# Stick-breaking attention with long and short query tiles paired in cycles, on one Trainium2 core

## The reference, cut to what matters

```python
u = rmsnorm(h, attn_norm_g)
q, k, v = split(u @ w_in)                      # 8 heads x 64
for each block of 128 queries (t0, t1 = t0 + 128):
    z = q[t0:t1] @ k[:t1].T * 64 ** -0.5
    strict = key index < query index
    sp = where(strict, softplus(z), 0)
    excl = reversed_cumsum(sp) - sp
    a = where(strict, exp(log_sigmoid(z) - excl), 0)
    out[t0:t1] = a @ v[:t1]
```

## Time and profile before

| what | us |
|---|---|
| median of three runs (4183.0 to 4185.79) | 4183.62 |
| the profiled execution, its own time | 4179.88 |
| its span, first to last instruction | 4178.1 |
| PE busy over the span | 3749.1 (90%) |
| ACT busy | 1303.3 (31%) |
| DVE busy | 1785.5 (43%) |
| POOL busy | 1304.8 (31%) |
| mean granted TensorE clock | 0.934 |

### The profile page before, as it was taken

How to read it: one execution, slowest core, us unless ns; L and a number is a source line. 1 busy time by engine, 2 the same in 40 slices (tenths; PEclk the granted TensorE clock), 3 DMA queues, 4 the chain that set the end, 5 groups by cost and what they waited for, 6 DMA issues and landing times. The chain is left out here.

```text
span 4178.1 us, 49886 instructions
## 1 busy us (share of the span) xinstructions
PE 3749.1 (90%) x17244; PEld 2990.7 (72%) x17244; DVE 1785.5 (43%) x3304; ACT 1303.3 (31%) x2355; POOL 1304.8 (31%) x777
## 2 busy tenths in 40 slices
PE   6877579688999999499999999998798999999897
PEld 4666556377888887378888888887686777768576
DVE  4555543424333323445555656565404233232332
ACT  3555423201011101245555555555301202020210
POOL 2110020013333332156555565655332221213031
PEclk8888589898999999699999999999898999999998
DMA  3111100122111110332443222520412111102051
GB/s 111 41 25 25 32 24 11 66 85 62 45 50 45 50 50 13 93 42 50 46 53 51 39 38 38 38 35 16 145 62 101 36 55 30 60 25 70 27 175 65
DMA packets 218590, 221.97 MB, mean 53 GB/s; under 512 B 12912, under 2 KB 174960, under 8 KB 218496
## 3 DMA queue, kind: packets, MB, share of 16 engines
q1 hardware_dynamic: 194160, 153.11, 16.9%
q10 hardware_dynamic: 24336, 67.64, 4.8%
HBM read 178.72 MB, written 33.62 MB: 51 GB/s over the span
## 5 line engine op out<-in xcount | busy, mean ns | idle before, releaser
L1191 POOL TENSOR_SCALAR even_probs<-even_probs,even_stat 128x128 f32<-128x128 f32 (+7 forms) x256 | 442.1, 1734 | 330.8 <-DVE even_stat L1568 330.8
L502 PE MATMUL ps<-all_u_hi,even_w_hi 128*128 128x512 f32 x1024 | 426.3, 416 | 24.7 <-POOL even_w_lo L1183 24.7
L506 PE MATMUL ps<-all_u_hi,even_w_lo 128*128 128x512 f32 x1024 | 403.2, 394 | 0.0
L505 PE MATMUL ps<-all_u_lo,even_w_hi 128*128 128x512 f32 x1024 | 400.9, 392 | 0.0
L455 POOL CAST odd_w_hi<-odd_w_raw 128x1024 fp32r<-128x1024 f32 x80 | 89.4, 1117 | 895.1 <-PE ps L502 686.7
L1573 DVE TENSOR_TENSOR even_probsT_lo<-ps,even_probsT_hi 128x512 fp32r<-128x512 f32 (+3 forms) x384 | 213.3, 556 | 280.2 <-ACT even_probsT_hi L1422 278.4
L502 PE MATMUL ps<-all_u_hi,odd_w_hi 128*128 128x512 f32 x768 | 305.5, 398 | 5.6 <-DVE ret_yT L2577 3.7
L505 PE MATMUL ps<-all_u_lo,odd_w_hi 128*128 128x512 f32 x768 | 303.2, 395 | 0.0
L506 PE MATMUL ps<-all_u_hi,odd_w_lo 128*128 128x512 f32 x768 | 303.1, 395 | 0.0
L1413 ACT ACTIVATE even_probs<-even_probs,even_stat 128x128 f32<-128x128 f32 (+7 forms) x256 | 199.1, 778 | 315.1 <-DVE even_stat L1562 315.1
L502 PEld LDWEIGHTS ps<-all_u_hi,even_w_hi 128*128 128x128 f32 x1024 | 194.5, 190 | 59.3 <-POOL even_w_lo L1183 25.1
(11 more groups left out here) (395 smaller groups left out, 8571.3 us busy)
## 6 DMA issues: line engine op xcount, KB each, us to landing
even_w_raw<-in_even_w_in_dram SPq DMA_DIRECT2D x64, 512.0 KB, 8.5
odd_w_raw<-in_odd_w_in_dram SPq DMA_DIRECT2D x48, 512.0 KB, 3.8
mlp_w_raw<-in_w_up_dram SPq DMA_DIRECT2D x32, 512.0 KB, 4.0
mlp_w_raw<-in_w_down_dram SPq DMA_DIRECT2D x32, 512.0 KB, 3.7
scratch_h<-residual SPq DMA_DIRECT2D x2, 4096.0 KB, 17.3
even_bias<-scratch_negc ACTq DMA_DIRECT2D x16, 512.0 KB, 6.7
scratch_yt<-even_yT ACTq DMA_DIRECT2D x32, 256.0 KB, 2.0
we_y_raw<-scratch_yt ACTq DMA_DIRECT2D x16, 512.0 KB, 4.3
```

The source lines that it names most:

```text
L502: ins = nc.tensor.matmul(dst, lh, rh, start=first, stop=False)
L505: nc.tensor.matmul(dst, lh, rl, start=False, stop=False)
L506: return nc.tensor.matmul(dst, ll, rh, start=False, stop=last)
L1191: nc.gpsimd.tensor_scalar(PB[g % 2][:, at], PB[g % 2][:, at], inv[:, s:s + 1], None, ALU.mult)\
```

## The change

`pair_stage` goes and `stick_stage` takes its place; the order of the units becomes k, q, v. No stage behind it is edited.

- **Cycles.** The two kinds of query tile of a head are paired: long rows 4, 5, 6, 7 (5 to 8 key tiles) with short rows 3, 2, 1, 0 (4 to 1 key tiles). A cycle is one long and one short row, 9 key tiles in all; a pair of heads has 8 cycles, the stage 32. The cycles run on over the borders of heads and pairs, and all is written out, without a hardware loop.
- **Three half-turns.** A cycle has three turns h: the long row's tiles 1 to 4, its tiles 5 to 8, and the short row. All go through one PSUM bank (`T`), and ACT alone copies them out, into a ring of three buffers.
- **Asked ahead.** Scores and `soft` of the long row stand two cycles ahead, of the short row one cycle; `probs` of the long row one cycle ahead. Long rows have two PSUM areas of two banks, the short row one bank.
- **Dense eighths.** Dense work for the next pair is cut into 24 eighths of 6 matmuls, one for each turn of the 24 in a pair (two at turns 2 and 5, none at 22 and 23).
- **High and low parts.** The eight DMAs go. ACT writes the high part of k to the other half of the partitions and the high part of q to the same half, DVE writes q's low part, POOL writes k's high part and its low part; the low part of k is zero on the other half.
- **Rows and v.** The short and long rows gather in one bank and ACT takes them out every second cycle (four copies a pair; before, 16 on DVE). v has two buffers and is turned through the dense bank, at the last two turns of the pair before. The rows go out by two DMAs for a pair.

```diff
-    def pair_stage(stage, kinds, rounds, weight, units, bases, w=None):
+    def stick_stage(stage, rounds, weight, bases, w):
...
+        SL = [ps[:, 0:2, :].rearrange("p b c -> p (b c)"), ps[:, 2:4, :].rearrange("p b c -> p (b c)")]
+        SS = ps[:, 4, :]
+        T = ps[:, 5, :]
+        O = ps[:, 6, :]
         DENSE = ps[:, 7, :]
...
+        def rows_of(long, c):
+            return 4 + c % 4 if long else 3 - c % 4
...
+        PIECES = [1] * STEPS
+        PIECES[2] = PIECES[5] = 2
+        PIECES[22] = PIECES[23] = 0
...
             @block.gpsimd
             def _(pool):
...
+                    nc.gpsimd.tensor_copy(KHH[m, hh, :], KN[m, :]).then_inc(doubled.sem, 1)
+                    pool.wait_ge(doubled.sem, doubled.at(n + 1))
+                    nc.gpsimd.tensor_tensor(KLO[m, hh, :], KN[m, :], KHH[m, hh, :].bitcast(F32), ALU.subtract)\
+                        .then_inc(doubled.sem, 1)
...
             @block.tensor
             def _(pe):
...
+                def turn(h):
+                    long, c, js = blocks_of(h)
+                    if js[0] == 0:
+                        pe.wait_ge(probs_ready.sem, probs_ready.at(index(long, c) + 1))
+                    if h:
+                        pe.wait_ge(probs_out_act.sem, probs_out_act.at(h))
+                    for i, j in enumerate(js):
+                        last = nc.tensor.transpose(T[:, i * P:i * P + P], probs_of(long, c)[:, j * P:j * P + P], ident[:])
+                    last.then_inc(probs_turned.sem, 1)
...
+                for e in range(4 * ND):
+                    eighth(0, e, ps[:, e // 4, :])
+                pe.wait_ge(dense_out.sem, dense_out.at(ND))
+                pe.wait_ge(step_pool.sem, step_pool.at(2))
+                scores(LONG, 0)
+                scores(LONG, 1)
+                scores(SHORT, 0)
+                turn_v(0, 0)
+                turn_v(0, 1)
+                for h in range(3 * NCY):
+                    c, k = divmod(h, 3)
+                    nxt = following(h)
+                    turn(h)
+                    if k == 0 and exists(c + 2):
+                        scores(LONG, c + 2)
+                    if k == 2 and exists(c + 1):
+                        scores(SHORT, c + 1)
+                    if h and k != 1:
+                        weigh(h - 1)
+                    for e in eighths_at(h) if nxt else ():
+                        if e % 4 == 0:
+                            pe.wait_ge(dense_out.sem, dense_out.at(ND * nxt + e // 4))
...
+                        eighth(nxt, e, DENSE)
+                    if k == 1:
+                        weigh(h - 1)
+                    if nxt and h % STEPS >= STEPS - 2:
+                        turn_v(nxt, h % STEPS - (STEPS - 2))
+                weigh(3 * NCY - 1)
...
             @block.scalar
             def _(act):
...
-                def duplicate(pair):
-
-                    act.wait_ge(dense_out.sem, dense_out.at(nd * pair + 4))
-                    for src, dst in ((QN, Q2), (KN, K2)):
-                        for hh in range(2):
-                            for part in range(2):
-                                act.dma_start(dst[part * SB_DIM:(part + 1) * SB_DIM, hh, :],
-                                              src[hh * SB_DIM:(hh + 1) * SB_DIM, :]).then_inc(doubled.sem, 16)
...
+                for n in range(ND):
+                    take_half(0, n, ps[:, n, :])
+                    if n == 1:
+                        split_of(0, 0, 0)
+                    elif n == 3:
+                        split_of(0, 0, 1)
+                soft(LONG, 0)
+                soft(LONG, 1)
+                soft(SHORT, 0)
+                split_of(0, 1, 0)
+                split_of(0, 1, 1)
+                probs(LONG, 0)
+                for h in range(3 * NCY):
+                    c, k = divmod(h, 3)
+                    nxt = following(h)
+                    s = h % STEPS
+                    if nxt and s:
+                        for e in eighths_at(h - 1):
+                            if e % 4 == 3:
+                                take_half(nxt, e // 4, DENSE)
+                    probs_out(h)
+                    if k == 0:
+                        if exists(c + 2):
+                            soft(LONG, c + 2)
+                        if exists(c + 1):
+                            probs(LONG, c + 1)
+                    elif k == 1:
+                        if c % 2 == 0 and c:
+                            rows_out(c - 1)
+                        probs(SHORT, c)
+                    elif exists(c + 1):
+                        soft(SHORT, c + 1)
+                    if nxt and s in (9, 14, 21, 22):
+                        split_of(nxt, s // 21, (9, 14, 21, 22).index(s) % 2)
+                    if s == 3 and h >= STEPS:
+                        store(h // STEPS - 1)
+                rows_out(NCY - 1)
+                store(rounds - 1)
...
             @block.vector
             def _(dve):
...
+                for h in range(3 * NCY):
+                    c, k = divmod(h, 3)
...
+                    if k == 0:
+                        later(SHORT, c)
+                    elif k == 1:
+                        if exists(c + 2):
+                            later(LONG, c + 2)
+                    if nxt and s == 15:
+                        split_lo_of(nxt, 0)
+                    if nxt and s >= STEPS - 2:
+                        v_rows(nxt, s - (STEPS - 2))
+                    if nxt and s == STEPS - 1:
+                        split_lo_of(nxt, 1)
...
-    bases = [0, SB_WIDTH, 2 * SB_WIDTH]
+    bases = [SB_WIDTH, 0, 2 * SB_WIDTH]
...
-    pair_stage("sb", ["sb"], SB_HEADS // 2, one(w_in), "qkv", [bases], w=w)
+    stick_stage("sb", SB_HEADS // 2, one(w_in), bases, w)
```

More of the change, by code:

```diff
@@ L638, in _ @@
+                split_keys(0, 0)
+                split(1, 0)
+                split_keys(0, 1)
+                split(1, 1)
+                split(1, 2)
+                for p in range(1, rounds):
+                    split(p + 1, 0)
+                    split_keys(p, 0)
+                    split(p + 1, 1)
+                    split_keys(p, 1)
+                    split(p + 1, 2)
             @block.tensor
             def _(pe):
-                if not ahead:
-                    w_open_pe(pe, w, opening=False)
@@ L643, in quarter, with eighth @@
-                def quarter(pair, i, dst):
-                    n, part = i // 2, i % 2
-                    u, half = halves[n]
-                    if half == 0 and part == 0:
-                        w_arrived(pe, w, pair, per, u)
+                def eighth(p, e, dst):
+                    n, piece = e // 4, e % 4
+                    u, half = n // 2, n % 2
+                    if half == 0 and piece == 0:
+                        w_arrived(pe, w, p, per, u)
                     tiles = w_tiles(w, u)
@@ new lines, in scores @@
+                def scores(long, c):
+                    hh = head_of(c)
+                    if long and c % 4 == 0:
+                        g = c // 4
+                        pe.wait_ge(split_hi.sem, split_hi.at(2 * g + 2))
+                        pe.wait_ge(split_lo.sem, split_lo.at(g + 1))
+                        pe.wait_ge(doubled.sem, doubled.at(2 * g + 2))
+                    before = c - 2 if long else c - 1
+                    if before >= 0:
+                        pe.wait_ge(scores_taken.sem, scores_taken.at(index(long, before) + 1))
+                    qt = rows_of(long, c)
+                    S, at, n = scores_of(long, c), slice(qt * P, qt * P + P), width(long, c)
+                    for c0 in range(0, n, HALF):
+                        c1 = max(min(c0 + HALF, n), c0 + 2 * P)
+                        nc.tensor.matmul(S[:, c0:c1], QHL[:, hh, at], KHH[:, hh, c0:c1], start=True, stop=False)
+                        nc.tensor.matmul(S[:, c0:c1], QHL[:, hh, at], KLO[:, hh, c0:c1], start=False, stop=True)
+                    nc.tensor.matmul(S[:, n - P:n], ident16[:], mask_strict[:], start=False, stop=True,
+                                     skip_group_check=True).then_inc(scores_ready.sem, 1)
```

585 lines of the change are left out of this document (210 added, 375 removed).

## The result

The changed kernel takes **4084.95 us** (median of four runs, 4084.06 to 4086.41) against 4183.31 us (4179.57 to 4185.79, four runs) for the kernel before on the same chip. The ratio is 0.9765, with a 95% interval of 0.975 to 0.9781: 98 us less, where 91 were forecast. The profiled execution has a time of its own of 4084.06 and a span of 4082.3, which is 95.8 us less than the span before.

The account below looks back on a forecast made before the run. A ring of hand-overs, with no engine full, was taken as the bound. Start 95, 24 dense cycles 242, last pair 77 and 1 for the end give 415 us: saving 91, time 4092, range 4052 to 4132.

Parts of the forecast that it names:

- The dense cycle: One of 24 cycles with dense work: 10.1 us, bounded by PE's floor of 8.6 and by 12.1.
- the ring: PE from short turn to long scores, 3.8 us, then ACT to `probs` short, 4.6; with hand-overs and short turn 8.85.
- high parts: In dense cycles, three of four high parts fall behind a long `soft` on ACT: 0.4 us a cycle.
- turn 10's wait: The next eighth waits for a dense half's take behind `probs` long, delaying the short turn: 0.25 us a cycle.
- doubled eighths: The doubled eighths at turns 2 and 5 lie in the serial part: 0.35 us a cycle.
- The last pair: Eight cycles without dense work: 7.5 us each at full clock, 10.1 at half; 9.6 taken, 77 us in all.
- What was costed at nothing: Single turn bank, POOL's splits of k, two row DMAs, and `later` with 3.9 us of slack a cycle: no cost.
- POOL: Some 2 us lost per POOL operation beside a DVE scan, five a pair: at most 1.3 us a cycle, within slack.
- A: Hand-overs vanish, PE at full clock bounds: dense cycle 8.7 us, saving 141, time 4043; chance 0.13 with what lies towards it.
- B: Asking ahead gains little and the clock dips as now: dense cycle 12.1 us, saving 32, time 4152; chance 0.22.
- C: Clock falls to half in dense cycles and stays: 17 us a cycle, slower by 75, time 4259; chance 0.035.
- D: The new order has no effect, 107 us a pair stays: only 4183 would come out; chance 0.015.

Follow-up runs that it names:

- e2: Changed kernel with six more dense eighths a pair moved from behind the long row's second half to the short turns: 4116.42 us.
- e12: e9 without its 96 unread matmuls in the last pair, everything else alike: 4045.89 us, ratio 0.967 to the kernel before.
- e7: Kernel before, with the eight DMAs of each pair issued from SP's queue instead of ACT's: 4163.42 us.
- e9: Changed kernel with rows copied before `probs` long, halves taken early, `probs` short first, high parts moved, no eighths at short turns, 96 unread matmuls: 4041.68 us.
- e10: Changed kernel with three of a pair's four high parts on ACT moved to turns without a long `soft` before them: 4074.89 us.
- e4: Changed kernel with a dense half that ends in a cycle's first turn copied out in that turn, before `probs` long: 4080.20 us.
- e5: Changed kernel with `probs` of the short row made before `probs` of the next long row: 4066.67 us.
- e6: Changed kernel with 96 matmuls that nobody reads added on PE in the last pair: 4076.21 us.
- e8: Changed kernel with DVE running each long row's scan twice: 4100.05 us.

## Why the prediction was right, step by step

- **What bounds the kernel.** That the order of the hand-overs between PE and ACT sets the time, and not the amount of work: e2 shows it for the changed kernel (+31.5 us from order alone), and e12 from the other side, 39 us quicker with the same work. For the kernel before it is read from the waits, and e7 tests one piece of it.
- **The dense cycle**, forecast 10.1 (bounds 8.6 to 12.1), measured 10.14: 243.4 us for 24 in place of 242. The hit is partly luck, since the cycle is not made up as drawn. The prediction closes the ring where PE waits for `probs` short, and in the dense cycles that wait is 0.5 us in all. PE stops elsewhere, for the take of a dense half (8.0), for the bank of the rows (6.4) and for the turned v (5.3): 20.6 us, 0.86 a cycle. The waits for the rows' bank and for v have no term in the sum. The other 9.28 us of a cycle PE is busy, where in e9, at a clock of 0.96 to 1.00, it is busy 8.75: some 0.5 us is the price of the lower level, which the sum, at full clock, leaves out. And the base of the ring, 8.85, lay so near PE's own 8.6 that the size of a cycle could not tell them apart; only the experiments do. ACT's work was 59.7 to 60.0 us a pair in place of 62. Of the terms tried alone, high parts 0.4 (e10: 0.37) and turn 10's wait 0.25 (e4, with the other takes of its kind: 0.23) came out at their size, `probs` long, 0.89, at less than half (e5: 0.40). The 0.35 of the doubled eighths stays open.
- **The last pair**, forecast 77 (9.6 a cycle, by leaning to the end at half clock), measured 74.1 (9.3) at 0.64. The fast end holds: at 0.97 a cycle was 7.6 (e6) where 7.5 stood. No run has this pair wholly at half clock, so the slow end, 10.1, is not tested by itself; an estimate from both ends fits, since a mean of 0.64 is 72% of the time at the lower level, and 7.5 + 0.72 x 2.6 = 9.4. Here PE does wait for `probs` short, as drawn (7.9 us), and for the rows' bank (11.2), which has no term. The Trainium skill (TensorE: Matmul & The Clock Gate, What's actually happening) says that throttled is the default state and activity releases it; e6's pair, which got faster when PE got more to do (0.64 to 0.97), agrees.
- **Start and end**: first turn forecast at 95, measured 94.41; store forecast at 415, measured 411.88. The last pair with the last copy took 3.9 us less than its 78 and the start 0.6 less; the dense cycles took 1.4 more. The forecast of 4092 missed the median by 7 us: those 3, 1.8 behind the stage, and the rest because the profiled execution lay 0.9 us below the median and not 3.7.
- **What was costed at nothing.** ACT's waits for `later` are 0, as said. The slack behind that was stated too large: e8 took 76.5 us of it in place of the 3.9 x 32 = 125 us that the text allows, and 15 us showed. A mean slack hides that POOL's work falls on a few cycles.
- **POOL**: bounded at 2 us for each of its operations beside a scan, five in a pair. DVE was busy 53.7 us in pair 1 and 49.5 in pair 2, which has no weight splits. The 4.2 us are two scans that waited, 2.1 at 246.00 and 1.9 at 251.48, and 0.2 at 224.93. So a single wait can pass the 2 us a little, but only two of the five subtractions caused one, and the pair's sum is far inside the bound. The Trainium skill (GPSIMD Engine Reference, Specifications) says that the two contend when a DVE instruction reads two inputs from SBUF; the scans at 246.00 and 251.48 agree. It doesn't make the bound stand at every overlap, as the prediction has it: the scan at 205.71 lost nothing, and POOL 0.2 us.
- **The rivals.** A (PE at full clock is the bound) is not the changed kernel, but e9 shows that it can be had by moving ACT's work: a cycle of 9.05 for its 8.7. B's price per cycle, 12.1, is near what e2 brought about (11.77). C, the clock falling and staying down, didn't happen at 0.93 and over; e2's 0.86 is a step towards it, and its cycle stayed below the 13.9 from which the change would lose. (From 8.6 and 17 us, 13.9 is a cycle with some 63% of the work at the lower level, not 55.) Stops of a microsecond were expected in the dense cycles; turn 10's was 2.7. D is out, and its 6.9 us of DMA issue a pair held (e7: 21 us in three pairs).
- **The signs named**: 79.3 us between the stores of the rows of pairs 1 and 2 (issued at 273.24 and 352.56), forecast as 79 to 83; ACT busy 60 for 62; clock 0.93, at the edge of the one forecast. Wrong was the list of largest waits: ACT for the turns holds, but PE's largest is that for the rows over the stage and that for the take in the dense cycles, and not that for `probs` short.
- **The range.** Its lower end, 4052, is called halfway to A; halfway between 4092 and 4043 is 4067. The 4084.95 lie inside either.

What stays open: the single profiled executions differ in the clock of one and the same code (69.2 to 74.5 us for the last pair), so gains of a few us could be placed in a pair only where medians and profile agree.

## What to carry to other kernels

When no engine is full, write down which instructions lie one behind the other in the ring of hand-overs, in program order on each engine, and count a shared bank's emptying among them. Then move every instruction that nobody asks for yet out of the stretch that the partner waits through: the same work in a better order was worth 39 us here (e12), in a worse one it cost 31. And look for queues that an engine fills for others: eight DMA issues a pair on ACT cost 21 us in the kernel before, and moved to SP's queue they cost nothing that the time shows (e7).

## What the runs showed of the hardware

- PE that stops more often pays twice. In e2 stops for `probs` short grew from 8.4 to 25.0 us over the stage, and the clock fell from 0.97 to 0.86 in the third pair. In e6 96 unread matmuls made a pair 13.4 us shorter in the profile, at a clock of 0.97 for 0.64.
- After the stop of 2.66 us that ended at 212.66 dense matmuls started 0.43 us apart, from 218.20 on again 0.235 apart.
- A DVE scan that begins while POOL's subtraction runs is held back for nearly the rest of it: 2.56 in place of 0.42 us for one tile, 3.61 in place of 1.76 for six, beside POOL operations of 2.37 and 2.35 us. A scan that begins first is hardly held (0.42 us at 205.71, 2.25 for 2.02 at 224.93), and POOL's operation is the one that grows: 2.58 and 3.99 us.
- POOL's subtraction on 64 partitions took 2.37 us, that on 128 partitions 2.35, each with a scan waiting: half the partitions saved it nothing.
